# Scaling the sample's rows of the feed-forward norm right behind their turned copy, in a two-layer decoder step

## What is computed

```python
def hier_moe(x, g2, r_g, r_e, w_gate, w_up, w_down):
    h = rmsnorm(x, g2).reshape(b * t, d)
    pg = softmax(h @ r_g); gi = argmax(pg); gw = max(pg)
    le = (h @ r_e).reshape(-1, N_GROUPS, E_PER)
    tw, ti = lax.top_k(softmax(le of group gi), TOP_K)
    gates = one_hot(gi * E_PER + ti) * gw * tw / sum(tw)
    a = silu(h @ w_gate[e]) * (h @ w_up[e]) * gates
    return sum over e of a @ w_down[e]
```

## Time and profile before

| | |
|---|---|
| median of 3 runs | 972.13 us (970.58 to 972.36) |
| profiled execution, its own time | 974.02 us |
| its span, first to last instruction | 972.3 us |
| around the span | 1.7 us |
| TensorE busy | 924.1 us, 95% of the span |
| VectorE, ScalarE, GpSimd busy | 396.7, 245.8 and 189.7 us |
| mean granted TensorE clock | 0.981 of full |

### The profile page before, as it was taken

How to read it: one execution, slowest core, us unless ns; L and a number is a source line. 1 busy time by engine, 2 the same in 40 slices (tenths; PEclk the granted TensorE clock), 3 DMA queues, 4 the chain that set the end, 5 groups by cost and what they waited for, 6 DMA issues and landing times. The chain is left out here.

```text
span 972.3 us, 13913 instructions
## 1 busy us (share of the span) xinstructions
PE 924.1 (95%) x5114; PEld 447.2 (46%) x5114; DVE 396.7 (41%) x1007; ACT 245.8 (25%) x493; POOL 189.7 (20%) x263
## 2 busy tenths in 40 slices
PE   9999999999997999999899999999999969999991
PEld 5444445556445443333544345455564444333330
DVE  2403235676465663111432212556673744621114
ACT  3202346642011021111131124656221111111110
POOL 2333201331100111110134031023220011111100
PEclk9999999999997999999999999999999979999996
DMA  9716004341017799998671150235110449999976
GB/s 341 282 38 270 1 1 136 93 169 44 22 44 274 291 413 397 400 406 356 241 268 55 63 208 1 88 92 169 61 33 22 171 161 382 414 388 406 421 272 229
DMA packets 39197, 197.51 MB, mean 203 GB/s; under 512 B 7096, under 2 KB 7224, under 8 KB 23248
## 3 DMA queue, kind: packets, MB, share of 16 engines
q1 hardware_dynamic: 19456, 136.03, 35.2%
q0 software_dynamic: 15312, 45.72, 13.7%
q10 hardware_dynamic: 4352, 14.76, 4.2%
HBM read 176.20 MB, written 28.84 MB: 211 GB/s over the span
## 5 line engine op out<-in xcount | busy, mean ns | idle before, releaser
L713 PE MATMUL ps<-ring,hT 128*128 128x512 f32 (+3 forms) x1312 | 397.1, 584 | 0.9 <-ACT ring L1404 0.6
L713 PEld LDWEIGHTS ps<-ring,hT 128*128 128x128 f32 (+2 forms) x1312 | 150.5, 152 | 197.3 <-issue 193.8
L713 PE MATMUL ps<-ring,cat 128*128 128x512 f32 (+2 forms) x560 | 181.8, 597 | 0.0
L713 PEld LDWEIGHTS ps<-ring,cat 128*128 128x128 f32 (+2 forms) x560 | 65.7, 157 | 81.0 <-issue 79.3
L2117 DVE TENSOR_TENSOR hT<-ps,par 128x512 f32<-128x512 f32 x52 | 33.7, 685 | 152.7 <-PE ps L711 149.8
L654 POOL DMA_INDIRECT y_rows<-hn,isca x26 | 26.3, 1011 | 231.8 <-ACT hn L1482 227.3
L533 POOL TENSOR_TENSOR st<-st,half 128x1 f32<-128x1 f32 (+3 forms) x60 | 63.3, 1055 | 11.0 <-POOL st L531 10.8
L531 POOL TENSOR_SCALAR st<-st 128x1 f32<-128x1 f32 (+3 forms) x60 | 15.6, 260 | 226.2 <-DVE st L1592 82.3
L1592 DVE TENSOR_REDUCE st<-sqj 128x8 f32<-128x512 f32 x20 | 13.4, 681 | 111.5 <-ACT sqj L1316 111.5
L713 PE MATMUL ps<-hT,ring 128*128 128x512 f32 x128 | 57.1, 599 | 0.7 <-DVE tmp L1649 0.7
L1482 ACT COPY hn<-ps 128x1024 f32<-128x1024 f32 x24 | 24.3, 1012 | 95.6 <-PE ps L713 95.6
(11 more groups left out here) (278 smaller groups left out, 1133.5 us busy)
## 6 DMA issues: line engine op xcount, KB each, us to landing
ring<-in_w SPq DMA_DIRECT2D x84, 1024.0 KB
kc<-in_w SPq DMA_DIRECT2D x10, 1024.0 KB
vc<-in_w SPq DMA_DIRECT2D x10, 1024.0 KB
v<-in_w SPq DMA_DIRECT2D x10, 1024.0 KB
kva<-in_w SPq DMA_DIRECT2D x10, 1024.0 KB
kc<-in_ck POOLq DMA_DIRECT2D x32, 256.0 KB, 3.7
vc<-in_cv POOLq DMA_DIRECT2D x32, 256.0 KB, 3.3
h_rows<-qk ACTq DMA_DIRECT2D x10, 512.0 KB, 2.6
```

The source lines that it names most:

```text
L713: ins = pe.matmul(out, lhsT, rhs, start=start, stop=stop, skip_group_check=loose)
```

## The change

VectorE's multiplication of the sample's rows with their root is moved up in VectorE's list, from behind `by_size()`, `chosen(TP)` and `add_out(0, TP - 1)` to right behind `turned(TP)`. No instruction is added or removed, and no wait is changed; the list of every other engine stays as it is.

```diff
@@ -1950,12 +1950,12 @@
                 add_sample_out()
                 chosen(2)
                 turned(TP)
+                scaled(TP)
                 higher_of(2)
                 lower_of(2)
                 by_size()
                 chosen(TP)
                 add_out(0, TP - 1)
-                scaled(TP)
                 higher_of(TP)
                 lower_of(TP)
                 turned(TP - 1, (0,))
```

## The result

The changed kernel took 965.68 us (median of 6 runs, 963.23 to 967.49), the kernel before 971.79 us beside it (970.58 to 972.36). The ratio is 0.9938 with a 95% interval of 0.9922 to 0.9954: 6.1 us less, where 8.0 were forecast. Two more comparisons of the same pair gave 0.9923 (0.9905 to 0.9941) and 0.9933 (0.9918 to 0.9947). The change makes the kernel some 0.7% faster.

What follows compares the result with a forecast made beforehand. TensorE, busy 95%, was held by 13.7 us of waits for the first gather. Gains of 3.3 + 5.5 + 0.2 = 9.0 us gave 965.0 from the profile, 963.1 from the median; 964.1 us was taken, range 960.0 to 968.0.

Steps and rivals of the forecast that it cites:

- The multiplication and its neighbours: VectorE's list behind `turned(TP)`: operand ready, no new wait; the displaced neighbours up to 0.67 us later, at no cost.
- The store: ScalarE's store of the sample's rows: goes at 287.8 instead of 293.60, lands in 2.6 us at 290.4.
- The gather's start: GpSimd's first gather starts 1.0 us behind its list `ifirst`, at 299.6 and 776.8 instead of 303.12 and 782.46.
- From its start to TensorE: First gather's start to TensorE's start on its rows: 4.5 and 4.3 us in the two layers, plus 0.2 each.
- The lower bound: Gather's start to TensorE's start with no weights moving: 4.50 and 4.33 us, against some 8.3 inside a weight stream.
- The 0.2 us for descriptor writing: GpSimd's descriptor writing for the gather, now beside VectorE's work: 0 to 0.45 us longer, 0.2 taken.
- The sum for the two waits: TensorE's two waits for the first gather: gains of 3.3 and 5.5 us in the two layers.
- The clock: TensorE's clock at the first turning: still falls; 0.1 us saved per layer, up to 1.7 if it returned early.
- nothing gives the gain back: Behind the first gather: later steps move up with TensorE, no weight-piece wait, next listed wait only 2.2 us.
- A: Rival: the first gather is held up inside the weight stream, 8.3 us; 1.4 us gained, 970.7 us; chance 0.07.
- B: Rival: the gather lands last of the DMA backlog, taking the store's 8.4 and 10.5 us; 975.4 us; chance 0.03.
- C: Rival: ScalarE's store held up, or another TensorE wait takes the gain; 969 us or no change; chance 0.06.

## Why the prediction was right, and where its size was off

**The multiplication and its neighbours: right.** The root was there, no wait arose. `add_out` moved by 0.15 us and the weight pieces by 0.32, each 0.22 more against the offset (0.37 and 0.54): under the 0.67 that I allowed, since VectorE had had small waits in between that took up the rest.

**The store: right.** Forecast for 287.8, it went at 287.3; ScalarE's queue issues it beside the last copy, not behind its end. It landed 3.3 us later, not 2.6, well before the list was there. The kernel with the late store shows that the store's place is the cause, and that VectorE's order adds nothing to it.

**The gather's start: right,** 1.04 us behind the list for a forecast of 1.0.

**From its start to TensorE: right in the first layer, short in the second.** The lower bound, 4.4 us, held in the first (4.38). The second took 5.12 us here and 4.9 in the two other profiles, where the kernel before has 4.33, 4.41 and 4.45. It is not the stream's end, as the kernels with weights held back took 4.9 and 5.15 too. The extra lies behind the gather's last packet. In the second layer that packet ends 4.0 to 4.25 us after the start in all of these profiles, before and after, but TensorE starts 0.9 us behind it instead of 0.4. In all six profiles with the extra (the one with the 8 matmuls and the third piece held is the sixth, 5.05 us) an instruction fetch, on queue q14, ends within 0.1 us of the gather's last packet. In those without it the fetch ends over 2 us earlier. That it is the cause is not shown. The 0.2 us for descriptor writing was not needed, nor did the 1.5 us come that the prediction worked out for a whole VectorE instruction lost in each layer: the row says 1.17 us before and after, with two VectorE instructions beside it in the first layer.

**The sum for the two waits: right.** The forecast was 8.8 us, the profile shows 3.6 + 4.9 = 8.5.

**The clock: nearly nothing, as taken.** It was low (0.50) for 10.2 us in each layer before and for 6.8 us after, but the turning lies inside the low stretch both times. From the turning's start to the first expert it is 7.39 us in both layers after, and 7.53 and 7.39 before.

**What failed is the step "nothing gives the gain back", and the sum's hold on the median.** First, the next wait in the list, the 2.2 us that I passed over, sits at the last expert slots, on matmuls that read the tile `v`, which a late weight piece fills:

```profile
450.74 0.63 PE L713 MATMUL ps<-v,hT 128*32 128x512 f32 x3 [1.20 <-SPq L167]
```

That is the kernel before. The last of the piece landed at 450.60. So TensorE does wait for weights there, by up to 1.2 us, contrary to my sentence. In the profile after it was shorter, not longer, so it took nothing back. Second, the layer's end took 1.6 us back in the first profile, and nothing in the two others. Third and largest: the profiled executions differ by 9.2, 10.1 and 9.2 us (974.0, 973.2 and 973.4 against 964.8, 963.1 and 964.1), just the forecast's 9.0, and the medians by 6.1, 7.5 and 6.2. The step that didn't hold is to take what single profiled executions differ by for what the medians differ by. The first profile of the kernel before, 974.0 us, lies above all six of its runs (970.6 to 972.4 us), and the profiled execution of the changed kernel was each time the fastest or second fastest of its six, which lie 3 to 4 us apart. An unprofiled execution leaves no trace, so at which place the others lose the 2 to 3 us isn't shown. The changed kernel's medians lie 0.9, 1.7 and 2.2 us above its profiled executions, those of the kernel before 2.2 and 0.5 us below and level. The four kernels with matmuls ahead have both within 0.6 us of each other. That may point at the clock behind the wait, as does the lower mean clock of the slower executions (above, for the late store), but the kernel with only the third piece held, whose clock falls too, doesn't fit (0.8 us below), so it stays open.

**The rivals.** A had the right mechanism for a gather inside a stream and too low a price, 8.3 us for a measured 10.1: with that price it would have made the kernel slower, not the same, as the weights behind the store did. The gap between A and the forecast is only when the stream ends: the changed kernel's was through at about 301 us, 1.6 us after the gather began, and the measured one's at about 308, 9 us after. B's landing time didn't occur with the store early. C's second half, another wait that takes over, is what happened when all weights were held.

## What to carry to other kernels

When an engine waits for a gather, ask what the gather itself waited for and what was queued ahead of that: here a store of 0.5 MB took 8 to 11 us behind 3 MB of weights and 3 us ahead of them, and a multiplication of 0.7 us, moved within its list, decided which. A transfer on the way to the critical engine wants its moment with short queues; holding back a bulk stream for it moves the collision to the next one. A sum from one profile told the mechanism here well and the median's gain by 2 to 3 us too much, so compare medians, look at how far single executions lie apart, and look at each wait in the list before calling it something else.

## What the runs showed of the hardware

A short transfer issued behind a long stream on another queue doesn't get its share at once. The gather's 0.38 MB, in the kernel with the weights behind the store, moved nothing for 3.8 us while the weights' queue ran at 103.7%, and then both moved together. Its first packet came 4.35 us after its start, where with empty queues it is 1.8 to 1.9 us. The store of the kernel before took 8.4 and 10.5 us for 0.5 MB; its first packet came 4.0 and 3.7 us after its issue, and 0.8 us after it in the changed kernel. The Trainium skill ("DMA: Bandwidth & Descriptors", section "Queues, rings and completion order") says that each engine takes turns between the queues it has work for; the second of the two stretches agrees (55.7%, 20.1% and 18.1% for three queues at once). The first doesn't, as to the 2.5 us by which the gather's first packet came later than with empty queues.

TensorE's granted clock fell to 0.50 at this place between 0.6 us before TensorE's wait for the gather began and 2.8 us after that, in the first layer of the changed kernel at 301.6 us, 0.1 us after. Where the idle piece was 2.2 to 3.0 us long it was low for 6.8 us in nine cases and for 3.4 in one. Where it was 5.7 to 8.1 us long it was low for 10.2 us in eight cases, for 13.7 in one and for 6.8 in one. Filled with 2 us of matmuls without a use, stretches of 2.7 and 3.1 us left it at 1.00 in the kernel with the third piece held; with the 8 matmuls alone it held in the first layer and fell in the second.
